# Moving tiles and results walked backwards, and split weights interleaved, in a one-core hybrid encoder layer

## What is computed

```python
u = rms_norm(h, norm_pre)
qa, ka, va, za, qg, kg, vg, zg, lr, ga, gg = split_cols(u @ w_in)
oa = attn_prompt(...)            # or attn_sample: window of 128, GQA, sinks
y_a = (oa * jax.nn.silu(za)) @ w_branch_attn
log_a = jax.nn.log_sigmoid((lr @ w_forget_up + b_forget)) / GLA_TAU
og, new_state = gla_mix(qg, kg, vg, log_a, state)
og = rms_norm(og, gla_norm).reshape(B, T, GLA_DV)
y_g = (og * jax.nn.silu(zg)) @ w_branch_gla
merged = jax.nn.sigmoid(ga + b_gate[:D_MODEL]) * y_a + jax.nn.sigmoid(gg + b_gate[D_MODEL:]) * y_g
h = h + rms_norm(merged @ w_out, norm_post)
```

## Time and profile before

| | |
|---|---|
| median of three runs | 2768.17 us (2767.89 to 2768.52) |
| profiled execution, its own time | 2767.97 us |
| its span, first to last instruction | 2766.2 us |
| mean granted TensorE clock | 0.997 |
| PE busy | 2719.7 us, 98%, 20948 matmuls |
| PEld busy | 2576.6 us, 93%, 20948 loads |
| DVE busy | 2095.7 us, 76% |
| ACT busy | 1212.0 us, 44% |
| DMA, mean | 166 GB/s |

### The profile page before, as it was taken

One profiled execution on the slowest core, in us unless ns is written; L12 is line 12 of the kernel. 1 busy time (PEld: TensorE's weight loads), 2 busy tenths in 40 slices (PEclk: granted clock), 3 DMA queues, 4 the chain that ended last, 5 costly groups with the idle time before them and its releaser, 6 DMA issues. The chain is left out here.

```text
span 2766.2 us, 51790 instructions
## 1 busy us (share of the span) xinstructions
PE 2719.7 (98%) x20948; PEld 2576.6 (93%) x20948; DVE 2095.7 (76%) x3346; ACT 1212.0 (44%) x2001; POOL 68.7 (2%) x48
## 2 busy tenths in 40 slices
PE   8999999999999999999999999999999999999999
PEld 8999999999999999999777887878799999999999
DVE  8999778778788877877777777677676787645566
ACT  6444333445354333344556666565532232433233
POOL 0221000000000000000000000000000000000000
PEclk9999999999999999999999999999999999999999
DMA  4565333436343333344656655565644746545567
GB/s 164 179 206 190 130 132 120 135 125 237 110 145 126 130 126 131 116 139 130 189 172 184 184 178 175 177 189 156 207 155 160 252 155 229 185 145 168 164 213 232
DMA packets 237456, 459.26 MB, mean 166 GB/s; under 512 B 23968, under 2 KB 142880, under 8 KB 236208
## 3 DMA queue, kind: packets, MB, share of 16 engines
q1 hardware_dynamic: 237232, 456.13, 50.5%
HBM read 367.01 MB, written 89.59 MB: 165 GB/s over the span
## 5 line engine op out<-in xcount | busy, mean ns | idle before, releaser
L2428 PE MATMUL bank<-th,w_split 128*128 128x272 f32 x4640 | 893.4, 289 | 0.7 <-DVE stage L1855 0.4
L2428 PEld LDWEIGHTS bank<-th,w_split 128*128 128x128 f32 x4640 | 731.3, 188 | 4.3 <-issue 3.1
L2428 PE MATMUL bank<-tl,w_split 128*128 128x272 f32 x2320 | 664.1, 286 | 0.0
L2406 PE MATMUL bank<-uh,w_split 128*128 128x272 f32 x2048 | 438.7, 300 | 12.5 <-DVE w_split L1590 7.6
L2428 PEld LDWEIGHTS bank<-tl,w_split 128*128 128x128 f32 x2320 | 436.3, 188 | 1.0 <-issue 1.0
L1124 ACT ACTIVATE w_split<-w_more 128x1024 fp32r<-128x1024 f32 x232 | 245.9, 1060 | 409.8 <-PE bank L2428 213.2
L1590 DVE TENSOR_TENSOR w_split<-w_raw,w_split 128x1024 fp32r<-128x1024 f32 x192 | 234.6, 1222 | 208.8 <-ACT w_split L1109 208.5
L2406 PEld LDWEIGHTS bank<-uh,w_split 128*128 128x128 f32 x2048 | 337.4, 191 | 54.4 <-issue 40.1
L2428 PE MATMUL bank<-uh,w_split 128*128 128x272 f32 x1856 | 367.6, 289 | 1.5 <-DVE stage L1744 1.5
L1603 DVE TENSOR_TENSOR w_split<-w_more,w_split 128x1024 fp32r<-128x1024 f32 x232 | 291.6, 1257 | 85.1 <-ACT w_split L1124 84.9
L1109 ACT ACTIVATE w_split<-w_raw 128x1024 fp32r<-128x1024 f32 x192 | 203.0, 1057 | 306.4 <-PE bank L2777 184.5
(11 more groups left out here) (296 smaller groups left out, 4132.3 us busy)
## 6 DMA issues: line engine op xcount, KB each, us to landing
w_raw<-in_w_tiles SPq DMA_DIRECT2D x328, 512.0 KB, 4.1
w_more<-in_w_tiles SPq DMA_DIRECT2D x120, 512.0 KB, 3.6
p_scratch<-stage SPq DMA_DIRECT2D x44, 544.0 KB, 3.0
gl<-p_scratch SPq DMA_DIRECT2D x24, 512.0 KB, 5.6
w_pair<-in_w_tiles SPq DMA_DIRECT2D x9, 1024.0 KB, 6.6
mixed_tokens_scratch<-xs SPq DMA_DIRECT2D x8, 1088.0 KB, 7.5
gate_scratch<-stage SPq DMA_DIRECT2D x16, 544.0 KB, 3.0
gate_scratch<-stage SPq DMA_DIRECT2D x64, 136.0 KB, 4.3
```

Of the source, the lines that this page charges most:

```text
L2406: ins = pe.matmul(out[:, 0:w], wt[:, h, k, :], ut[:, h * HK + k, 0:w], start=start and k == 0 and j == 0, stop=stop and k == HK - 1 and j ...
L2428: ins = pe.matmul(out[:, 0:GAW], wt[:, k], ut[:, k], start=start and k == 0 and i == 0, stop=stop and k == HK - 1 and i == 2, skip_group_c ...
```

## The change

The file gains one helper and changes three sets of access patterns. Engine by engine, the instructions and their order stay the same; only lines move by up to three.

- The views of the weight parts take every second element: high parts at 0, 2, 4, ..., 254, low parts at 1, 3, ..., 255 of the 272. So ACT writes with a step of two elements, DVE reads the high part and writes the low one with a step of two, and TensorE's weight loads read with a step of two. The raw weights stay contiguous.
- In all matmuls with split weights up to the output groups, the moving tile is read from its last column to its first, and the bank is written from its last column to its first. Column c of the tile still goes to column c of the bank.
- The last stage keeps contiguous halves of `w_split` (its list `last_w` is spelled out) and forward patterns.

```diff
-        w_hi, w_lo = w_split[:, :, :, 0:P], w_split[:, :, :, P:2 * P]
+        w_hi, w_lo = (w_split[:, :, :, i:2 * P:2] for i in range(2))
...
-            w_hi2, w_lo2 = w_split2[:, :, 0:P], w_split2[:, :, P:2 * P]
+            w_hi2, w_lo2 = (w_split2[:, :, i:2 * P:2] for i in range(2))
...
-        last_w = [(w_raw_b, w_hi_b, w_lo_b), (w_raw, w_hi, w_lo)]
+        last_w = [(w_raw_b, w_hi_b, w_lo_b), (w_raw, w_split[:, :, :, 0:P], w_split[:, :, :, P:2 * P])]
...
+            def backwards(tile):
+                return tile[:, ::-1]
+
             def products(out, h, hi_t, lo_t, w, done, start, stop, ks=range(HK)):
...
-                        ins = pe.matmul(out[:, 0:w], wt[:, h, k, :], ut[:, h * HK + k, 0:w],
+                        ins = pe.matmul(backwards(out[:, 0:w]), wt[:, h, k, :], backwards(ut[:, h * HK + k, 0:w]),
...
-                        ins = pe.matmul(out[:, 0:GAW], wt[:, k], ut[:, k], start=start and k == 0 and i == 0,
+                        ins = pe.matmul(backwards(out[:, 0:GAW]), wt[:, k], backwards(ut[:, k]), start=start and k == 0 and i == 0,
...
-                        ins = pe.matmul(bank[2 * (e % 2) + FIRST_BLOCKS[b][1]][:, 0:GAW], wt[:, k], ut[:, k], start=e < 2 and k == 0 and i == 0,
+                        ins = pe.matmul(backwards(bank[2 * (e % 2) + FIRST_BLOCKS[b][1]][:, 0:GAW]), wt[:, k], backwards(ut[:, k]), start=e < 2 and k == 0 and i == 0,
...
-                        ins = pe.matmul(bank[2 * (e % 2) + th][:, 0:GAW], wt[:, k], ut[:, k], start=e < 2 and k == 0 and i == 0,
+                        ins = pe.matmul(backwards(bank[2 * (e % 2) + th][:, 0:GAW]), wt[:, k], backwards(ut[:, k]), start=e < 2 and k == 0 and i == 0,
...
-                            ins = pe.matmul(out[:, 0:GAW], wt[:, k], ut[:, g * BLK + k], start=start and k == 0 and j == 0,
+                            ins = pe.matmul(backwards(out[:, 0:GAW]), wt[:, k], backwards(ut[:, g * BLK + k]), start=start and k == 0 and j == 0,
...
-                        ins = pe.matmul(bank[r][:, 0:GRP[g][1]], wt[:, h, k, :], ut[h * HK + k][:, 0:GRP[g][1]],
+                        ins = pe.matmul(backwards(bank[r][:, 0:GRP[g][1]]), wt[:, h, k, :], backwards(ut[h * HK + k][:, 0:GRP[g][1]]),
```

## The result

The changed kernel takes 2785.32 us in the median of four runs (2783.42 to 2788.87), the kernel before 2768.03 us (2767.34 to 2768.52): a ratio of 1.0063, 95% interval 1.0051 to 1.0074. It is 17.3 us slower, a small loss, but clear of the spread of the runs.

A forecast was written before the change was run, and what follows sets the result against it. The prediction took TensorE, fed without holes at 0.443 ns a column, as the bound. Backward reads, backward writes, interleaved loads and splits each added 0 to 2768 us, giving 2768 us, with a range of 2762 to 3436 us.

The forecast's parts named there:

- the likeliest case: All four changed patterns, at the matmuls and splits, are free or hidden: 2768 us, chance 0.49.
- What bounds the kernel: TensorE, 98% busy and fed without holes: a matmul costs almost nothing but its columns, 0.443 ns each.
- the last lines of the prediction: A price on each matmul would make the forecast wrong; each 1 ns of it is 17.5 us.
- the load side: 17472 weight loads reading every second word: taken at 0, hidden up to 125.7 ns under 272-column matmuls, 189.5 under 416.
- The reason given for that 0: A weight load asks for 128 words in 111.7 ns, against 272 in 125.7 ns on the moving side.
- The upper bound of 223 ns: Weight load if each word costs a fetch that now serves two: 2 x 111.7 = 223.4 ns.
- Backward walks: Moving tiles read and results written in falling order in 17472 matmuls: 0 each, at most 0.886 ns a column.
- The doubled-columns rival: Backward columns cost double in the matmuls' read or write: 2203 us more, 4971 us, chance 0.16.
- Splits: ACT and DVE splitting weights with a step of two: 0 to 440 ns more a split, hidden by DVE's free 0.557 us.
- the 0.43 ns a jump: From line 2309's writes, 3 ns for 7 jumps; at one jump for each of 1024 elements, +440 ns a split.
- the rival that DVE grows past its air: DVE's splits outgrow their free 0.557 us a product: 3015 us at a doubled element, down to 2774; chance 0.20.
- The two pages on DVE: For DVE's step-two splits, one page gives +0 (2768 us), the other an estimated +672 ns a split, +47 us (2815).

## Why the prediction was wrong

It forecast no change with 2768 us, and gave slower 0.48. The measured 2785.3 us is inside the stated range, which says little of a range that reaches to 3436. The loss is clear of the noise, and the likeliest case is not what happened. (The range also leaves out 0.16 + 0.06 = 0.22 of the chances, not the 0.2 it allows itself; nothing hangs on it.)

- **What bounds the kernel: right.** TensorE is at its columns' pace and has no slack. That is why a nanosecond a matmul is seen in full, as the last lines of the prediction said: 17472 matmuls make 17.5 us of each nanosecond. The reading was right and the price of 0 wrong.
- **The step that failed is the load side.** That all up to 125.7 ns is hidden treats the load as free until it is the longer of two. The occupancy rose to about 120 ns, below the limit as required, and each pair still grew by 0.7 to 1.9 ns (loads alone; 2.2 at 416 columns). The term was taken at 0 and measured 14.6 us. Neither the 6 ns of air at 272 columns nor the 70 at 416 made a full cover.
- **The reason given for that 0** was that a load asks for a word at half the moving side's pace. That pace didn't protect it. What counts is how far the words lie apart: about 120 ns at a step of two, 176 at three, 234 at four. The upper bound of 223 ns was of the right size for a step of four.
- **Backward walks: right**, 0 for both sides, measured +0.5 us (-2 to +3). The doubled-columns rival, at 0.16, got no support in any kernel, and neither did the rule on non-contiguous patterns that the Trainium skill gives on "PSUM — Partial Sum Buffer", section "Specifications (TRN2)": with results alone written backwards the ratio was 1.0000 (0.9991 to 1.0009), so a falling walk does not behave as one of those.
- **Splits: a price of 0 to 440 ns, hidden, was right in kind.** DVE paid 0 to 3 ns in the changed kernel, so the 0.43 ns a jump from the earlier trace rows does not scale up to a jump an element, and the rival that DVE grows past its air, at 0.20, did not come. ACT paid 90 to 146 ns. The two together cost 2.4 us (0.3 to 5.3), which the forecast had at 0; by what wait they cost it is not shown.
- **The two pages on DVE.** The Trainium skill's rule on "SBUF — State Buffer", section "SBUF: two separate sides", that two hits in a 16-byte line keep the full rate, agrees with DVE here: 1223 to 1225 ns with a step of two, 2043 with a step of four. The Trainium skill's rule on "Vector Engine (DVE) Microarchitecture Reference", section 5.2, that only adjacent pairs do, does not fit a step of two, where by the prediction's sum it would have been an estimated 1.89 us a split. The measurement decides for the first.
- **What stays open.** Why a load that needs less time than its matmul lengthens the pair at all. At 272 columns the small air is a likely reason, since one slow load in three costs as much as three there. But at 416 columns, where a load of about 120 ns has 70 ns of air, the pair grew by 2.2 ns too (294.45 us for 291.11, loads alone). Some sharing of the read side between load and moving tile would fit; no run isolates it. Whether the load's price goes with 16-byte pieces touched or with distance is open as well. Pairs of neighbours in a load were not tried, nor a step above four.

## What to carry to other kernels

Where TensorE is fed without holes, ask of every change in an access pattern what it adds to one load or one matmul, and multiply by their number: work that runs beside a matmul can cost a nanosecond or two of each even where it is shorter than the matmul, and once it is the longer it costs the whole difference. Keep split weights contiguous: with a step of two float32 elements this kernel is 0.6% slower, with three in the loads 28%, with four in loads and splits 64%. Walking tiles and banks backwards cost nothing that the device time shows (+0.5 us, -2 to +3).

## What the runs showed of the hardware

- A weight load of 128 float32 columns occupies its path for at most 112 ns contiguous, about 120 with a step of two elements, 176 with three and 234 with four (236 beside 416 columns); its recorded duration is 188, 195, 263 and 330 ns. From three to four that is 58.3 ns more, which is 1.82 ns for each further 16 bytes touched, or 58 ns for an element of step; the runs don't tell the two apart.
- A load that is shorter than the matmul beside it still lengthened the pair: by 0.7 ns at 272 columns in the first stage, 1.9 in the branch stage and 2.2 at 416 columns.
- DVE's subtraction of 1024 elements takes 1.22 us with a step of two on one source and the destination, and 2.04 us with a step of four. ACT's copy takes 1.06 us contiguous, 1.15 to 1.16 with a step of two or in pairs (1.20 beside backward walks), and 2.06 to 2.09 with a step of four.
- A bank written from its last column to its first takes the same time as forward (ratio 1.0000). A moving tile read so takes the same time at 272 columns (125.6 ns for 125.7), and 1.6 ns more at 416, with contiguous weights.
